# Three experts kept out of the scatter-add, tile roots in batches, and the overflow list spread over five experts

## The reference, cut to what matters

```
h   = h + sum over the row's two experts e of  w_e * (silu(xf @ w_gate[e]) * (xf @ w_up[e])) @ w_down[e]
y   = h * rsqrt(mean(h*h) + 1e-6) * norm_final_g
```

## Time and profile before

| | us |
|---|---|
| median of three runs | 1858.48 |
| lowest and highest | 1855.87, 1858.67 |
| span of the profiled execution, first to last instruction | 1853.7 |
| PE busy in the span | 1785.6 |
| DVE, ACT, POOL busy | 1063.0, 780.6, 510.4 |

### The profile page before, as it was taken

One profiled execution on the slowest core, in us unless ns is written; L12 is line 12 of the kernel. 1 busy time (PEld: TensorE's weight loads), 2 busy tenths in 40 slices (PEclk: granted clock), 3 DMA queues, 4 the chain that ended last, 5 costly groups with the idle time before them and its releaser, 6 DMA issues. The chain is left out here.

```text
span 1853.7 us, 25673 instructions
## 1 busy us (share of the span) xinstructions
PE 1785.6 (96%) x10105; PEld 1550.8 (84%) x10105; DVE 1063.0 (57%) x1244; ACT 780.6 (42%) x918; POOL 510.4 (28%) x284
## 2 busy tenths in 40 slices
PE   8999999999999999999999979989999999999993
PEld 6989989999999999999999978857777777767772
DVE  7565580001455445554621142367888888889886
ACT  5455460000122111221300023227778878777875
POOL 0422322222222222222233310012233433323331
PEclk9999999999999999999999989999999999999997
DMA  4111111223111111111122366558999999999986
GB/s 149 38 52 52 32 55 61 73 73 117 49 38 34 37 37 44 41 34 37 39 87 95 120 208 225 210 203 307 366 380 369 379 369 371 378 368 379 366 318 236
DMA packets 146290, 316.24 MB, mean 171 GB/s; under 512 B 10986, under 2 KB 106314, under 8 KB 121496
## 3 DMA queue, kind: packets, MB, share of 16 engines
q1 hardware_dynamic: 135896, 287.74, 42.6%
q0 software_dynamic: 10304, 27.24, 5.3%
HBM read 287.72 MB, written 36.08 MB: 175 GB/s over the span
## 5 line engine op out<-in xcount | busy, mean ns | idle before, releaser
L222 PE MATMUL job_ps<-xn_hi,w_hi 128*128 128x352 f32 x1488 | 494.9, 333 | 0.3 <-issue 0.3
L224 PE MATMUL job_ps<-xn_hi,w_lo 128*128 128x352 f32 x1488 | 478.7, 322 | 0.0
L223 PE MATMUL job_ps<-xn_lo,w_hi 128*128 128x352 f32 x1488 | 478.0, 321 | 0.0
L206 POOL CAST w_hi<-w_raw 128x1024 fp32r<-128x1024 f32 x78 | 85.6, 1097 | 774.4 <-issue 467.3
L222 PEld LDWEIGHTS job_ps<-xn_hi,w_hi 128*128 128x128 f32 x1488 | 280.0, 188 | 4.1 <-issue 1.0
L223 PEld LDWEIGHTS job_ps<-xn_lo,w_hi 128*128 128x128 f32 x1488 | 280.6, 189 | 2.5 <-issue 0.3
L224 PEld LDWEIGHTS job_ps<-xn_hi,w_lo 128*128 128x128 f32 x1488 | 279.9, 188 | 0.0
L2289 DVE TENSOR_TENSOR ex_raw_lo<-ex_raw,ex_w_hi 128x2048 fp32r<-128x2048 f32 x88 | 200.0, 2285 | 13.4 <-ACT ex_w_hi L2192 13.3
L208 POOL TENSOR_TENSOR w_lo<-w_raw,w_hi 128x1024 fp32r<-128x1024 f32 x78 | 205.0, 2629 | 6.3
L2192 ACT ACTIVATE ex_w_hi<-ex_raw 128x2048 fp32r<-128x2048 f32 x88 | 168.8, 1918 | 57.1 <-PE ex_y L2066 24.5
L754 DVE TENSOR_TENSOR gate<-job_ps,gate 128x352 f32<-128x352 f32 x48 | 25.2, 525 | 288.6 <-PE job_ps L224 288.6
(11 more groups left out here) (327 smaller groups left out, 3379.9 us busy)
## 6 DMA issues: line engine op xcount, KB each, us to landing
ex_raw<-in_w_chunks SPq DMA_DIRECT2D x88, 1024.0 KB, 20.3
u<-in_w_chunks SPq DMA_DIRECT2D x52, 1024.0 KB, 17.8
raw_more<-in_w_chunks SPq DMA_DIRECT2D x52, 1024.0 KB, 19.3
w_raw<-in_w_in SPq DMA_DIRECT2D x64, 512.0 KB, 4.0
merged_lru<-gate SPq DMA_DIRECT2D x8, 528.0 KB, 5.2
spare<-merged_lru SPq DMA_DIRECT2D x8, 528.0 KB, 5.9
merged<-gate SPq DMA_DIRECT2D x8, 528.0 KB, 5.0
w_raw<-in_w_lru_o SPq DMA_DIRECT2D x8, 512.0 KB, 4.4
```

The costliest lines, as they stand in the source:

```text
L206: pool.tensor_copy(M.w_hi[s][:], M.w_raw[s][:]).then_inc(M.hi_done[s], 1)
L222: pe.matmul(out, M.w_hi[s][:, k, :], x_hi[:, k, cols], start=(k == 0), stop=False)
L223: pe.matmul(out, M.w_hi[s][:, k, :], x_lo[:, k, cols], start=False, stop=False)
L224: mm = pe.matmul(out, M.w_lo[s][:, k, :], x_hi[:, k, cols], start=False, stop=(k == KD - 1))
```

## The change

1. `ADDED` becomes E - 3: experts 29, 30 and 31 in the order (weights of experts 31, 7 and 15 of the model) stay out of the scatter-add. SP waits for the scatter-add of expert 28, and for `used` of each buffer that it fills. POOL gathers the h rows of three experts. Slot 29's scaled result in `y` is added by one DVE operation; the results of 30 and 31 as before. Behind the tiles stand six row stores instead of four; four of them wait for or stand behind the store of the last tile.
2. Roots and reciprocals are taken for tiles 0 to 2, 3 to 5 and 6 to 8 at once (the last batch with the rows of slot 29), then for the rows of each other slot.
3. In ACT's last step the squares of the first three tiles and the table load stand ahead of `hi(LAST, 4)`, and the squares of the next three behind `hi(LAST, 5)`.
4. The transposes of the last hidden rows move between the two chunks of expert 30's down product; their high and low parts go into the x buffers.
5. `weigh_over` is cut into five pieces, behind experts 16, 18, 20, 21 and 22; `weigh_over_rows` is behind 12 and 14 (before: 12 and 16), `sample_rows` behind 24 (before: 22).

```diff
-    ID = [e for e in range(E) if e != PER_GROUP - 1] + [PER_GROUP - 1]
+    ID = [e for e in range(E) if e not in (PER_GROUP - 1, 2 * PER_GROUP - 1)] + [PER_GROUP - 1, 2 * PER_GROUP - 1]
+    IN_SLOTS = (E - 3, E - 2, E - 1)
...
-        ADDED = E - 2
+        IN_SLOTS = Chunks.IN_SLOTS
+        ADDED = IN_SLOTS[0]
+        N_SLOTS = len(IN_SLOTS)
...
+        BATCHES = ((0, 3), (3, 6), (6, NTILE + 1), (NTILE + 1, NTILE + 2), (NTILE + 2, NTILE + 3))
...
         sp.wait_ge(y_added, 16 * ADDED)
-        for t in LAST_FIRST:
-            sp.dma_start(fin[t][0:n_rows(t), :], h_rows[span(t), :]).then_inc(h_in[t], 16)
+        for i, t in enumerate(LAST_FIRST):
+            sp.wait_ge(used, N_CHUNKS - RAW + 1 + (i if i < 4 else i + 2) // 2)
+            sp.dma_start(fin[i][0:n_rows(t), :], h_rows[span(t), :]).then_inc(h_in[i], 16)
...
         pool.wait_ge(sample_stored, 16)
-        for k, e in enumerate((ADDED, LAST)):
-            pool.wait_ge(rows_done, k + 1)
-            indirect(y_sample[0], router.sample_row[k], y[e % 2][0:SLOTS, :], None, DEC - 1).then_inc(rows_put, 16)
+        for k in range(N_SLOTS - 1):
+            put_sample(k)
         pool.wait_ge(out_stored, 16 * NT)
-        for e in (ADDED, LAST):
-            indirect(y_prompt[0], row[e % ROWS], y[e % 2][0:SLOTS, :], None, SEQ - 1).then_inc(rows_put, 16)
+        for k in range(N_SLOTS - 1):
+            put_prompt(k)
+        put_sample(N_SLOTS - 1)
+        put_prompt(N_SLOTS - 1)
...
-            elif s < E:
+            elif s < LAST:
                 down(s - 1)
+            elif s == LAST:
+                down(s - 1, lambda: turn_h(LAST))
...
+        def last_step():
+            act.wait_ge(ss_set, 1)
+            act.wait_ge(used, N_CHUNKS - RAW + 6)
+            hi(LAST, 3)
+            hi(LAST - 1, 4)
+            silu(LAST)
+            h_part(LAST - 1)
+            hi(LAST - 1, 5)
+            for i in range(3):
+                square_tile(i)
+            act.activation(warm[:], R.eps[0:1, :], ACT.Sqrt)
+            hi(LAST, 4)
+            root(0)
+            h_part(LAST)
+            hi(LAST, 5)
+            for i in range(3, 6):
+                square_tile(i)
+            root(1)
+            for i in range(6, NTILE):
+                square_tile(i)
+            square_rows(0, 1)
+            root(2)
+            square_rows(1, 1 + N2)
+            root(3)
+            square_rows(2, 1 + 2 * N2)
+            root(4)
...
-            if s in (12, 16):
-                router.weigh_over_rows(dve, s // 4 - 3)
+            if s in (12, 14):
+                router.weigh_over_rows(dve, s // 2 - 6)
+            if s == 16:
+                router.weigh_over_sum(dve)
+            if s == 18:
+                router.weigh_over_scan(dve)
             if s == 20:
-                router.weigh_over(dve)
+                router.weigh_over_place(dve)
+            if s == 21:
+                router.weigh_over_index(dve)
             if s == 22:
-                router.sample_rows(dve, (Chunks.ID[ADDED], Chunks.ID[LAST]))
-        lo(LAST, 4)
-        lo(LAST, 5)
-        h_part(LAST)
+                router.weigh_over_list(dve)
+            if s == 24:
+                router.sample_rows(dve, [Chunks.ID[e] for e in IN_SLOTS])
+            if s == 25:
+                dve.memset(ss[:], 1.0).then_inc(ss_set, 1)
...
+        dve.wait_ge(y_done, N2 * (ADDED + 1))
+        dve.wait_ge(rows_in[0], 16)
+        dve.tensor_tensor(base[0][0:SLOTS, :], base[0][0:SLOTS, :], y[ADDED % 2][0:SLOTS, :],
+                          ALU.add).then_inc(rows_added, 1)
+        lo(LAST, 4)
+        turned_round(0)
+        h_part(LAST)
+        lo(LAST, 5)
         dve.wait_ge(g_in, 16)
+        dve.wait_ge(used, AT[LAST - 1, 5] + 1)
+        for m in range(N2):
+            add_rows(1, m, py[m])
+        turned_round(1)
+        for i in range(6):
+            scaled_tile(i)
+        turned_round(2)
+        for m, src in enumerate((pg, pu)):
+            dve.wait_ge(used, AT[LAST, 4 + m] + 1)
+            add_rows(2, m, src)
+        for i in range(6, NTILE):
+            scaled_tile(i)
+        scaled_rows(0)
+        turned_round(3)
+        scaled_rows(1)
+        turned_round(4)
+        scaled_rows(2)
```

More of the change, by code:

```diff
@@ L1867, in experts @@
         al_stored = fsem("all_stored")
-        h_in = [fsem(f"h_in{t}") for t in range(NTILE)]
+        h_in = [fsem(f"h_in{i}") for i in range(NTILE)]
         g_in, st_stored, out_stored = fsem("g_in"), fsem("st_stored"), fsem("out_stored")
-        sq_done, rms_done, rstd_done, out_done = fsem("sq_done"), fsem("rms_done"), fsem("rstd_done"), fsem("out_done")
+        ss_set = fsem("ss_set")
+        sq_done, rms_done, rstd_done = fsem("sq_done"), fsem("rms_done"), fsem("rstd_done")
+        out_done = fsem("out_done")
         n_rows = lambda t: P if t < NT else DEC
         span = lambda t: slice(t * P, t * P + n_rows(t))
[L1873 to L1876, removed]
+        BATCHES = ((0, 3), (3, 6), (6, NTILE + 1), (NTILE + 1, NTILE + 2), (NTILE + 2, NTILE + 3))
+        batch_of = lambda at: [lo <= at < hi for lo, hi in BATCHES].index(True)
         out_rows = lambda t: y_prompt[0, span(t), :] if t < NT else y_sample[0]
@@ L2094, in turn_h, with down @@
             ins.then_inc(h_turned, 1)
-        def down(e):
+        def down(e, between=lambda: None):
             pe.wait_ge(h_lo_done, e + 1)
@@ L2099, in down @@
             for i, c in enumerate((4, 5)):
+                if i:
+                    between()
                 n = AT[e, c]
@@ L2123, in down_last @@
                         kk = 2 * i + k
-                        ins = three(out[0:SLOTS, :], h_hi[:, kk, :], h_lo[:, kk, :], hi[:, k, at], lo[:, k, at],
+                        ins = three(out[0:SLOTS, :], x[:, kk, :], x_low[:, kk, :], hi[:, k, at], lo[:, k, at],
                                     kk == 0, kk == KF - 1)
@@ L2227, in scalar, with square, square_tile, square_rows @@
         x_part(0)
+        def square(x, n, at, to=junk):
+            if at:
+                act.wait_ge(sq_done, at)
+            act.activation(to[0:n, :], x, ACT.Square, accum_out=ss[0:n, at:at + 1]).then_inc(sq_done, 1)
+        def square_tile(i):
+            n = n_rows(LAST_FIRST[i])
+            act.wait_ge(h_in[i], 16)
+            square(fin[i][0:n, :], n, i)
+        def square_rows(k, added):
+            act.wait_ge(rows_added, added)
+            square(base[k][0:SLOTS, :], SLOTS, NTILE + k)
+        def root(b):
+            lo, hi = BATCHES[b]
+            act.wait_ge(sq_done, hi)
+            act.activation(rms[:, lo:hi], ss[:, lo:hi], ACT.Sqrt, bias=R.eps[:], scale=1.0 / D).then_inc(rms_done, 1)
+        def last_step():
[24 more added lines that the diff above has]
+            root(4)
         for s in range(E):
@@ L2264, in behind @@
             for i, t in enumerate(LAST_FIRST):
-                root(al[t][0:n_rows(t), :], n_rows(t), t, al_sq, al_rms, i, raw[Chunks.FIRST][:, 0:D])
+                n = n_rows(t)
+                act.activation(raw[Chunks.FIRST][0:n, 0:D], al[t][0:n, :], ACT.Square,
+                               accum_out=ss[0:n, t:t + 1]).then_inc(al_sq, 1)
+                act.wait_ge(al_sq, i + 1)
+                act.activation(rms[0:n, t:t + 1], ss[0:n, t:t + 1], ACT.Sqrt, bias=R.eps[0:n, :],
+                               scale=1.0 / D).then_inc(al_rms, 1)
         def each(i):
@@ L2346, in add_rows, with turned_round @@
+            dve.scalar_tensor_tensor(out=base[k][0:SLOTS, at], in0=src[0:SLOTS, :], scalar=weight(IN_SLOTS[k]),
+                                     in1=base[k][0:SLOTS, at], op0=ALU.mult,
                                      op1=ALU.add).then_inc(rows_added, 1)
[L2348 to L2350 removed]
+        def turned_round(b):
+            lo, hi = BATCHES[b]
+            dve.wait_ge(rms_done, b + 1)
+            dve.reciprocal(rstd[:, lo:hi], rms[:, lo:hi]).then_inc(rstd_done, 1)
```

145 lines of the change are left out of this document (71 added, 74 removed).

## The result

The changed kernel takes 1867.95 us, the median of four runs (1865.42 to 1869.23), against 1858.27 us for the kernel before on the same chip. The ratio is 1.0054, with a 95% interval of 1.0040 to 1.0069: slower by 9.7 us. The prediction was 1866.0 us, within 1856 to 1869, with 74% on slower.

The account below looks back on a forecast made before the run. PE's matmuls, 17.7 us an expert, plus stalls, the end and a lagging weight queue. Third tile at 1820.5, S at 1821.7, plus 39.5 gives 1861.2, 7.5 over 1853.7; 1858.5 + 7.5 = 1866.0 us, range 1856 to 1869.

Parts of the forecast that it names:

- The new wait of ACT: ACT's last step: squares wait for the third tile and hold both conversions, DVE and PE; PE idles some 9 us.
- S: End of ACT's first three squares, just ahead of the table load: forecast at 1821.7, with the span ending 39.5 us later.
- The overflow list: Behind expert 20: cutting it removes a 4.9 us stall, but only 0.9 us is credited because the weight queue lags.
- Where ACT would wait: Small waits of ACT for weight chunks, expected in the last three or four experts.
- The landing of the last chunk: End of the weight queue: the last weight chunk still lands at 1815.2, as before the change.
- net two: POOL's queue at the end: three gathers more, one scatter-add less, taken to delay the third tile by 1.3 us.
- the prediction's upper bound: Cost of the net two gathers by share of time on the DMA engines: 2.6 us.
- the third tile: Last tile load that ACT's first squares need: 4.0 us of transfers behind the last chunk, landing forecast at 1820.5.
- What lies around the span: Time outside the profiled span, taken as an unchanged 4.8 us added to every span.
- A: Rival at the end: tiles are there in time, third before 1814; 1859 to 1860 us; chance 0.14 with part-way cases.
- B: Rival, faster: the DMA queue keeps up, so the 4.9 us of the overflow stall reach the end; 1854.9 us; chance 0.12.

Follow-up runs that it names:

- e9: The changed kernel as it is, timed again on another chip: 1868.41 us, ratio 1.0052 to the kernel before.
- e1: The kernel before with only the overflow list cut into five pieces: 1854.04 us, ratio 0.9995 to the kernel before.
- e7: The kernel before with slot rows spread over the partitions and the overflow list in five pieces: 1848.87 us, ratio 0.9961 to the kernel before.
- e3: The kernel before with only the slot rows spread over the partitions: 1851.09 us, ratio 0.9979 to the kernel before.
- e8: The changed kernel with empty lists for its three gathers of h rows: 1861.88 us, ratio 1.0032 to the kernel before.
- e4: The changed kernel with the slot rows spread over the partitions: 1847.74 us, ratio 0.9964 to the kernel before.
- e2: The changed kernel with ACT's first three squares behind both last conversions, DVE's first reciprocals later: 1861.43 us, ratio 1.0032 to the kernel before.

## Why the prediction was right

**The new wait of ACT.** Right, as placed: squares before the table load, both conversions behind them, DVE and PE behind those. The wait of PE was 6.9 us (8.0 in e9), for some 9 predicted. From S to the end the sum was 39.5 and the trace has 39.7. Two of its terms missed by as much as they made up for each other: DVE let the last tile go 0.7 us sooner than reckoned (S+21.9 for S+22.6), and that store needed 4.5 us to land and not 3.8. The rest was of about the right size, the four row stores and the slower clock of PE included. PE's granted clock was 0.73 from 1833.9 to 1844.6, part at the lower level, and it ended the product in time, as reckoned.

**The overflow list.** Right: the stall of 4.9 us was real, and the lagging queue took it back. e1 shows the second half (no gain, 27 waits for chunks), e7 against e3 the first, once the queue has slack (5.1 us on one profile each, 3.3 by their ratios).

**Where ACT would wait.** Off: expected in the last three or four experts, found from 1684.67 on, over some seven. The prediction's own figures would have said so. The slack that the earlier trace rows leave at 1646 is 35.3 - 26.3 = 9.0 us; without the stall ahead of it 4.9 less, 4.1; at 1.3 us an expert that is gone after three experts, at about 1700 (an estimate from these rows). PE's 10.4 us of waits for these chunks weren't in the sum as such.

**The landing of the last chunk.** This is the step that was mis-sized. The prediction had it at 1815.2, as before, since less than a chunk's slack was left; it came at 1822.1, 6.9 us later. The term of 1.3 us for the gathers ("net two") stands for the same thing, extra work of POOL's queue beside the backlog, and was too small. e8 puts all three gathers at 3.7 us by the ratios and 6.5 by the medians. By the prediction's upper bound, a share of time spread over all 16 engines (2.6 us for two), three would cost 3.9. That is inside what e8 measured, so whether the bound was too low as well isn't shown by the times. The prediction's own observation, that some engines are idle while others drain, should have led it to charge the gathers to the slow share alone, where the semaphore events of e8 put them. Between the last chunk and the third tile it was fair: 4.2 us for the 4.0 of the earlier trace rows with no gather in it. Sum for S: +6.9 for the chunk, -1.3 that was added behind it, +0.2 and +0.2: +6.0.

The Trainium skill (DMA: Bandwidth & Descriptors, Queues, rings and completion order) has an engine alternate between its queues packet by packet. By it the prediction weighed 2.6 us against its 1.3. The runs lean to that side: three gathers cost 3.7 or 6.5 us, and would cost 3.9 by the full share and 2.0 by the half that was taken.

**What lies around the span.** 4.8 us were added and 1.8 are there. The end of the span was 5.0 us too early for the median run (1867.95 - 1.8 = 1866.2 against 1861.2) and this term 3.0 too long, so the prediction missed by 2.0 us with the help of two errors of opposite sign, which is luck. Both have one source: the profiled execution before ended some 2.8 us under the median (1853.7 + 1.8 = 1855.5 for 1858.27), and that of the changed kernel 1.3 us above its own. Of the 6.0 us by which S was late against the prediction, 4.1 can come from that. Counted as a difference of medians, the change costs 9.7 us where 7.5 were predicted, a miss of 2.2.

**The rivals.** A and B both hung on whether the tiles are there in time, and that was the right fork. e4 is the other branch: with the rows spread it came to 0.9964, better than B (1854.9 of 1858.5 is 0.9981, just above the interval). Spreading the rows also gains something by itself, as e3 shows (0.9979).

**What stays open.** That the late share of a chunk is that of the engines which carry the filled slots, and that neighbouring partitions share an engine, was argued from e3 and e4 and not shown: the sixteen semaphore events show an uneven load and carry no engine's name. How the 9.7 us divide is known only in parts that overlap, since each run takes away one cause of a wait that has two: 4.1 us for ACT's order (e2), 3.7 to 6.5 for the gathers (e8), 0.90% for the whole lag (e4). The two row stores more are 2.4 us of it by their spacing; no run took them alone away.

## What to carry to other kernels

Read the time from issue to landing down the whole program beside the stretches in which the DMA engines are partly idle: if the one grows while the others show idle engines, the load is uneven, and the place of the rows in an indirect transfer may be worth more than a new order of the end (here 0.90% for the changed kernel, 0.22% for ACT's order). Price the removal of a stall against the slack of the queue that feeds the stage, and give it nothing if that queue is already late. An operation that waits for a transfer belongs behind all that an in-order engine still owes to others.

## What the runs showed of the hardware that was not expected

**The place of the rows sets the lag.** Same bytes, same instructions, other partitions: the last chunk's landing went from 34.4 to 11.4 us, and from 41.1 to 15.8.

**Issuing itself blocks.** The last chunk's issue took SP 7.93 us, and five tile loads took 20.76, in the changed kernel. SP's queue in e4, where the lag is gone:

```profile
1777.03 0.33 SPq L1818 DMA_DIRECT2D ex_raw<-in_w_chunks  x1
...
1794.87 2.54 SPq L1965 DMA_DIRECT2D u<-h_rows  x5
```

The same issues take 0.33 and 2.54 us. So a long issue in SP's timeline is a sign of a late queue, which the kernel before already showed for its last chunk (4.16 us at 1780.80) and which the prediction didn't use.

**A late transfer is late in a part of its shares.** In the kernel before, seven of the last chunk's sixteen semaphore events came by 1791.8 us and the last at 1815.2; three gathers beside it, in the changed kernel, moved the last to 1822.1 and left seven by 1793.7.
